# One query chunk of layer 0's second half is taken from the streamed place, and loads around it change their order and places

## The reference

```python
q = rmsnorm(qkv[..., :D]...); k = rmsnorm(qkv[..., D:2 * D]...); v = qkv[..., 2 * D:]
attn = p[:, :, 0] - lam * p[:, :, 1]            # two softmaxes a head
h = h + rmsnorm(attn @ v, sub_gain) * (1 - lam_init) @ w_o

q = (xt @ w_q).reshape(T, 8, 2, 128)            # PEER: 8 retrieval heads
s = einsum('thpd,hpkd->thpk', q, sub_keys)      # 128 keys in each half
s_top, i_top = top_k(s, 16); cand = all 256 sums of a head; best, pos = top_k(cand, 16)
gates = softmax(best); idx = i_top[half 0] * 128 + i_top[half 1]
act = gelu(u_tab[idx] . x) * gates; y = sum(act * v_tab[idx])
```

## Time and profile before

| | us |
|---|---|
| median of three runs | 1524.82 |
| profiled execution | 1526.51 |
| its span | 1524.5 |
| TensorE busy | 1347.4 |
| VectorE busy | 992.3 |
| ScalarE busy | 596.1 |
| GpSimd busy | 570.4 |

### The profile page before, as it was taken

The page is one execution under the profiler, slowest core; times in us unless marked ns, Lnnn a source line. Parts: engine busy times, 40 slices in busy tenths (PEclk is TensorE's granted clock), DMA queues, the critical chain, the costliest instruction groups (busy, mean ns, idle before and its releaser), DMA issues.

```text
span 1524.5 us, 12571 instructions
## 1 busy us (share of the span) xinstructions
PE 1347.4 (88%) x3294; PEld 573.2 (38%) x3294; DVE 992.3 (65%) x2411; ACT 596.1 (39%) x1805; POOL 570.4 (37%) x518
## 2 busy tenths in 40 slices
PE   9999899899878889889887899899979889877777
PEld 4444344344333334334332334343433333222222
DVE  4677877875656777456478546667567867764444
ACT  1334364643333434334334433343434344343333
POOL 0033334453323344344334434333434444343442
PEclk9999999999999999999999999999999999999999
DMA  9879999999999999999999999999999999999998
GB/s 390 342 290 421 359 424 419 421 415 420 423 422 424 416 415 395 422 420 414 422 411 408 420 420 420 420 406 422 409 421 419 414 416 421 413 408 422 421 420 334
DMA packets 85751, 621.82 MB, mean 408 GB/s; under 512 B 9520, under 2 KB 9648, under 8 KB 13104
## 3 DMA queue, kind: packets, MB, share of 16 engines
q0 software_dynamic: 74016, 536.90, 85.6%
q1 hardware_dynamic: 9936, 76.81, 12.2%
q10 hardware_dynamic: 1728, 7.31, 1.2%
HBM read 619.94 MB, written 1.05 MB: 407 GB/s over the span
## 4 chain that ended last, share of the span: by engine, by line
DMA 42%; PE 33%; DVE 13%; ACT 7%; issue 4%; POOL 1%; SPq 0%; DVEq 0%; POOLq 0%; ACTq 0%
DMA ring<-in_peer_uv_dram,idx 41%; PE acc L649 22%; PE pp L397 9%; DVE ring L1460 7%; ACT diag L993 2%; DMA ring<-in_w_qkv_dram 2%; ACT weight L989 1%; ACT L987 1%; ACT gelu L987 1%; ACT L850 1%; POOL ring L764 1%; PE tt L412 1%; ACT work L813 1%; DVE top_i L1177 1%; DVE pick L1219 0%
## 5 line engine op out<-in xcount | busy, mean ns | idle before, releaser
L649 PE MATMUL acc<-ring,diag 128*128 128x512 f32 x2048 | 995.2, 611 | 165.9 <-ACT diag L993 161.3
L1460 DVE CUSTOM_DVE_ANT_0 ring<-ring,xf 128x1024 f32<-128x1024 f32 x512 | 627.1, 1226 | 456.5 <-DMA ring<-in_peer_uv_dram,idx 447.2
L764 POOL DMA_INDIRECT ring<-in_peer_uv_dram,idx x510 | 566.2, 1110 | 937.4 <-PE acc L649 828.4
L649 PEld LDWEIGHTS acc<-ring,diag 128*128 128x128 f32 x2048 | 371.0, 191 | 726.0 <-ACT diag L993 383.6
L987 ACT ACTIVATE gelu<-dots 128x1 f32<-128x1 f32 x512 | 103.6, 202 | 803.4 <-DVE dots L1460 803.0
L993 ACT ACTIVATE diag<-const,weight 128x128 f32<-128x128 f32 x512 | 205.4, 401 | 16.8
L989 ACT ACTIVATE weight<-gelu,gates 128x1 f32<-128x1 f32 x512 | 150.8, 294 | 16.6
L397 PE MATMUL pp<-stream,xT 128*128 128x512 f32 x160 | 81.1, 596 | 0.0
L397 PE MATMUL pp<-stream,rows 128*128 128x512 f32 x96 | 49.0, 592 | 0.0
L397 PEld LDWEIGHTS pp<-stream,xT 128*128 128x128 f32 x160 | 30.4, 194 | 36.0 <-issue 36.0
L1460 DVE DVE_READ_ACCUMULATOR2_ANT dots<- 128x1 f32 x512 | 42.0, 82 | 0.0
(11 more groups left out here) (165 smaller groups left out, 763.8 us busy)
## 6 DMA issues: line engine op xcount, KB each, us to landing
stream<-in_peer_w_q_dram SPq DMA_DIRECT2D x18, 1024.0 KB, 9.4
stream<-in_conv_w_in_dram SPq DMA_DIRECT2D x12, 1024.0 KB, 9.4
ring<-in_peer_uv_dram,idx POOLq DMA_INDIRECT x510, 10.4
stream<-in_w_qkv_dram SPq DMA_DIRECT2D x4, 1024.0 KB, 11.9
ring<-in_w_qkv_dram SPq DMA_DIRECT2D x2, 2048.0 KB, 26.8
stream<-in_w_o_dram SPq DMA_DIRECT2D x4, 1024.0 KB, 18.5
kept<-in_peer_w_q_dram SPq DMA_DIRECT2D x2, 2048.0 KB, 11.5
ring<-in_w_qkv_dram SPq DMA_DIRECT2D x2, 1024.0 KB, 11.7
```

What stands on the lines that cost most here:

```text
L649: mm = nc.tensor.matmul(acc[half][:, :], diag[:, s % RING, :], row[:, D + half * 512:D + (half + 1) * 512], start=(k == 0), stop=(k == SLO ...
L764: nc.gpsimd.indirect_dma_start(dst, None, uv_dram, bass.IndirectOffsetOnAxis(idx[:, at:at + 1], 0)).then_inc(landed, 16)
L1460: nc.vector.tensor_tensor_reduce(row[:, 0:D], row[:, 0:D], xf[:, s // SLOTS % 2, :], 1.0, 0.0, ALU.mult, ALU.add, dots[:, s % RING:s % RIN ...
```

## The change

Query chunk 2 of layer 0 stays in the streamed place for both halves, as chunk 3 stays in `kept`. The second half ranks chunks 2 and 3 (heads 4 to 7) first and then 1 and 0 (`QUERY_ORDER`), and its gathers run over the heads in this order. For that, half 1's key chunk 1 is projected at slot 25 (was 41), query chunk 2 of half 0 at slot 33 (was 25), value chunk 1 at slot 41 (was 33) and query chunk 3 at slot 55 (was 50). The second output chunk of half 1 is loaded to place 6, where the V rows were, and its first four matmuls are due at slot 80 (was 72). Layer 1's first loads stand in another order and ahead of the second half's query chunks. The normalisation of key chunk 1 uses another scratch area and no longer waits for a transpose. The functions `chunk_of` and `reader_after` map a position to the chunk and to the reader.

```diff
--- before.py
+++ after.py
@@ -66,7 +66,7 @@
     dict(q0=12, k0=22, q1=30, k1=54,
          logits0=25, bias0=26, max0=30, exp0=31, diff0=35, turn0=38, values0=42,
          logits1=57, bias1=58, max1=62, exp1=63, diff1=68, turn1=71, values1=75,
-         norm0=45, norm1=77, gain=54, y0=49, y1=81, out00=68, out10=72, out01=84, out11=88, h0=88, f0=90, h1=92, f1=94, scale=93,
+         norm0=45, norm1=77, gain=54, y0=49, y1=81, out00=68, out10=80, out01=84, out11=88, h0=88, f0=90, h1=92, f1=94, scale=93,
          wq0=94, wq1=104, wq2=112, wq3=120),
     dict(x=2, in2=6, in4=14, in3=22, in5=30, in0=38, in1=46, z0=23, z1=39, turn_z0=25, turn_z1=41, turn_g0=49, turn_g1=57,
          conv0=28, conv1=44, gain=20, times0=52, times1=59, out00=60, out10=64, out01=68, out11=72, h0=72, f0=74, h1=76, f1=78,
@@ -77,17 +77,23 @@
 )
 SECOND_HEAD = 0
 FIRST_NORM = 8
-LATE_RANK_PROJECT = {1: 0, 2: 25, 3: 50}
+LATE_RANK_PROJECT = {1: 0, 2: 33, 3: 55}
+QUERY_ORDER = {1: (2, 3, 1, 0)}
 RANK_AT = {(1, 2): 133, (1, 3): 149}
 HALF = KT // 2
 RANK_PIECES = {(0, 1): 2, (0, 2): 2, (0, 3): 1, (1, 0): 2}
-LATE_IN_PROJECT = {2: 9, 1: 17, 5: 33, 3: 41}
-SHARED = {(1, "in", 0), (1, "in", 4), (1, "in", 5), (1, "out", 0), (1, "wq", 3),
+LATE_IN_PROJECT = {2: 9, 1: 17, 3: 25, 5: 41}
+SHARED = {(1, "in", 0), (1, "in", 4), (1, "in", 5), (1, "out", 0), (1, "wq", 0), (1, "wq", 1),
           (3, "in", 2), (3, "in", 3), (3, "in", 5), (3, "out", 0), (3, "out", 1), (3, "wq", 2), (3, "wq", 3)}
 PARTS = 2
 DEEP = KT // PARTS
 WARM = 3
 
+
+
+def chunk_of(n, what, c):
+
+    return QUERY_ORDER[n][c] if what == "wq" and n in QUERY_ORDER else c
 
 
 def pieces(n, c):
@@ -293,9 +299,9 @@
             places[2 + i] = ring[:, 2 * i:2 * i + 2, :].rearrange("p r d -> p (r d)")
         loads = [(0, "in", 0, 4), (0, "in", 2, 5), (0, "in", 1, STREAM), (0, "in", 3, 3), (0, "in", 4, 2), (0, "in", 5, 7),
                  (0, "out", 0, 8), (0, "out", 1, STREAM), (0, "wq", 0, 5), (1, "in", 2, HOLES), (1, "in", 1, 9), (0, "wq", 1, STREAM)]
-        loads += [(0, "wq", 2, STREAM), (1, "in", 3, STREAM), (0, "wq", 3, 7),
-                  (1, "out", 1, STREAM), (1, "wq", 0, STREAM), (1, "wq", 1, STREAM), (1, "wq", 2, STREAM)]
-        loads += [(2, "in", 2, 6), (2, "out", 0, 8), (2, "in", 4, STREAM), (2, "in", 3, 7), (2, "out", 1, 9), (2, "in", 5, 10), (2, "in", 0, STREAM),
+        loads += [(1, "in", 3, STREAM), (0, "wq", 2, STREAM), (0, "wq", 3, 7), (1, "out", 1, 6)]
+        loads += [(2, "out", 1, 9), (2, "out", 0, 8), (2, "in", 2, 6), (1, "wq", 2, STREAM), (2, "in", 3, 7), (1, "wq", 3, STREAM),
+                  (2, "in", 4, STREAM), (2, "in", 5, 10), (2, "in", 0, STREAM),
                   (2, "in", 1, STREAM), (2, "wq", 0, STREAM), (2, "wq", 1, STREAM)]
         loads += [(3, "in", 4, STREAM), (2, "wq", 2, 6), (2, "wq", 3, 7), (3, "in", 0, STREAM), (3, "in", 1, STREAM),
                   (3, "wq", 0, STREAM), (3, "wq", 1, STREAM)]
@@ -338,7 +344,13 @@
 
         def held(n, what, c):
 
-            return held_at[(n - 1 if (n, what, c) in SHARED else n, what, c)]
+            if (n, what, c) in SHARED:
+                return held_at[n - 1, what, chunk_of(n, what, c)]
+            return held_at[n, what, c]
+
+        def reader_after(n, what, c):
+
+            return next(((n + 1, what, later) for later in range(6) if (n + 1, what, later) in SHARED and chunk_of(n + 1, what, later) == c), None)
 
         def weights(n, what, c, k):
 
@@ -397,7 +409,7 @@
                     mm = nc.tensor.matmul(bank[:, 0:width], src[:, k, :], weights(n, what, c, k)[:, columns], start=(k == 0), stop=(k == KT - 1))
                     if k == KT - 1:
                         mm.then_inc(pool.written_sem(key), 1)
-                    elif k % DEEP == DEEP - 1 and held(n, what, c)[0] == STREAM:
+                    elif k % DEEP == DEEP - 1 and held(n, what, c)[0] == STREAM and reader_after(n, what, c) is None:
                         mm.then_inc(part_used, 1)
 
             def project(pool, n, what, c, src, at, ks=range(KT)):
@@ -469,7 +481,7 @@
                 key = (n, "score" + part, c)
                 bank = take(ss, key)
                 for j in range(2 * js[0], 2 * js[0] + 2 * len(js)):
-                    mm = nc.tensor.matmul(bank[:, j * P:(j + 1) * P], qT[:, j, :], keysT[:, 4 * c + j, :], start=True, stop=True)
+                    mm = nc.tensor.matmul(bank[:, j * P:(j + 1) * P], qT[:, j, :], keysT[:, 4 * chunk_of(n, "wq", c) + j, :], start=True, stop=True)
                 mm.then_inc(ss.written_sem(key), 1)
 
             def front():
@@ -653,8 +665,8 @@
                 mm.then_inc(v_used, 1)
 
             front()
-            sides = begun(late(1), late_input(2), turn_late("q", 0), late_input(1), turn_late("k", 0), attention(0), late(2),
-                          turn_late("q", 1), late_input(5), late_input(3), turn_late("k", 1), late(3), turn_mixed(0), attention(1), turn_mixed(1),
+            sides = begun(late(1), late_input(2), turn_late("q", 0), late_input(1), turn_late("k", 0), attention(0), late_input(3),
+                          turn_late("q", 1), late(2), late_input(5), turn_late("k", 1), late(3), turn_mixed(0), attention(1), turn_mixed(1),
                           output(1), turn_output(1), *(experts(1, c) for c in range(4)))
             for n in (2, 3):
                 sides += begun(gated_input(n), turn_gated(n), output(n), turn_output(n), *(experts(n, c) for c in range(4)))
@@ -669,12 +681,12 @@
         @block.sync
         def _(sp):
             def matrix_of(n, what, c):
-                return {"in": in_dram[n // 2], "out": out_w_dram[n // 2], "wq": peer_w_q[n // 2]}[what][c]
+                return {"in": in_dram[n // 2], "out": out_w_dram[n // 2], "wq": peer_w_q[n // 2]}[what][chunk_of(n, what, c)]
 
             def last_reader(n, what, c):
 
-                if (n + 1, what, c) in SHARED:
-                    n = n + 1
+                if reader_after(n, what, c):
+                    return reader_after(n, what, c)
                 return n, "wqb" if (n, what, c) == (0, "wq", 0) else what, c
 
             def load_first():
@@ -994,7 +1006,7 @@
 
             front()
             sides = begun(second_head(), late(1), late_input(2), turn_late("q", 0), late_input(1), turn_late("k", 0), attention(0),
-                          late(2), turn_late("q", 1), late_input(5), late_input(3), turn_late("k", 1), new_gain(1), late(3), turn_mixed(0),
+                          late_input(3), turn_late("q", 1), late(2), late_input(5), turn_late("k", 1), new_gain(1), late(3), turn_mixed(0),
                           attention(1), turn_mixed(1), output(1), *(experts(1, c) for c in range(4)), new_keys())
             for n in (2, 3):
                 sides += begun(gated_input(n), turn_gated(n), new_gain(n), output(n), *(experts(n, c) for c in range(4)))
@@ -1081,9 +1093,7 @@
 
                 copied(dve, pool, (n, "in", c))
                 src = mixed_rows(n, c).rearrange("p (c d) -> p c d", d=DH)
-                if (n, c) == (1, 3):
-                    written(dve, tt, (1, "attn", 1))
-                square_groups(src, 8, DH, rows[:, 0:CHUNK] if n == 1 and c < 3 else scratch[:, 0:CHUNK])
+                square_groups(src, 8, DH, rows[:, 0:CHUNK] if n == 1 else scratch[:, 0:CHUNK])
                 yield
                 rsqrt_of_mean(8, DH, root[:, 0:8])
                 yield
@@ -1462,7 +1472,7 @@
 
             front()
             sides = begun(*(finish(n) for n in range(WINDOWS - 1)))
-            sides += begun(second_head(), first_norm(), late_input(2), late(1), late_input(1), attention(0), late(2), late_input(3), late(3), attention(1),
+            sides += begun(second_head(), first_norm(), late_input(2), late(1), late_input(1), attention(0), late_input(3), late(2), late(3), attention(1),
                            output(1), *(experts(1, c) for c in range(4)))
             for n in (2, 3):
                 sides += begun(gated_input(n), convolve(n), output(n), *(experts(n, c) for c in range(4)))
```

## The result

The kernel after takes 1527.2 us (median of 20 runs) against 1524.97 us of the kernel before on the same chip: ratio 1.0015 [1.0009, 1.0021], 2.2 us slower. The forecast was 1522.2 us, 2.6 us faster. The profiled execution took 1530.85 us with a span of 1529.0, 3.6 us over the median of its own runs; places in the traces are read from single executions, times from the medians.

The account below looks back on a forecast made before the run. DMA bytes were taken as the first bound, with TensorE's pace almost equal in stretches without weight loads. The terms -5.0 + 2 + 0.4 = -2.6 us took the median from 1524.82 to 1522.2 us; range 1519.5 to 1527.5.

Parts of the forecast that it names:

- Part 1: Six weight chunks of 2.097 MB fetched instead of seven in this part of the list: 5.0 us gained at 421 GB/s.
- Part 2: Loads leave 200 to 245 us, so the DMA idles there: 2 us taken, between 0.9 and 3.6.
- Part 3: Heads 4 and 5 ranked at slots 46 to 53 instead of 38 to 45: cost 0.4 us, bounds 0 and 5.6.
- 1 to 2 of waits: Slots 55 to 68: TensorE's waits in us, added to 32.6 us of work, so slot 68 starts at 296 to 298.
- part 5: Loads moved to slots 79 to 92, DMA-bound still: 0, up to 1 us; key normalisation at slots 34 to 36: 0.
- Part 4: Short leads of query chunks and second output chunk before their use: 0 each, up to 1 us for some.
- The key normalisation, 0: 4 us of VectorE at slots 34 to 36, beside 4.48 us of waiting for ScalarE's exponentials: cost 0.
- Rival 3: VectorE becomes the bound in slots 46 to 76, slot 55 is 3.8 us late: 1528.6 us; chance 0.16.
- rival 2: Gain eaten: ranking and the exponentials after it keep slot 68 at 300 us, time 1524.8 us; chance 0.20.
- Rival 4: TensorE's clock falls in a wait for VectorE, 1.7 us per group of four add matmuls: 1523.9 us; chance 0.08.
- The two signs: Forecast wrong if slot 68 starts after 300 us, or more than 2.4 us of idling shows before slot 76.

Follow-up runs that it names:

- e3: Kernel after, but query chunk 2 is not shared and is fetched once more (2.097 MB, asked for at slot 75): 1532.88 us, 1.0052 of before.
- e2: Kernel after, with VectorE's normalisation of key chunk 1 begun at slot 37 instead of 34: 1525.39 us, 1.0001 of before.
- e8: Kernel after, with the second output chunk's first four matmuls due at slot 82 instead of 80: 1527.98 us, 1.0021 of before.
- e12: Kernel after, with value chunk 1 at slot 44, query chunk 3 at 57, heads 6 and 7 ranked from 72, normalisation in slot 34: 1525.7 us, 0.9997 of before.
- e10: e2 with value chunk 1 at slot 44, query chunk 3 at slot 57, heads 6 and 7 ranked from slot 72: 1523.15 us, 0.9986 of before.
- e6: Kernel after, with normalisation of key chunk 1 from slot 37 and ranking of heads 6 and 7 from slot 71: 1526.2 us, 1.0006 of before.
- e9: e2 with the projection of query chunk 3 at slot 53 instead of 55: 1525.5 us, 1.0002 of before.
- e11: e2 plus 2.1 MB of extra loads, asked for from slot 35 on and used by nothing: 1524.74 us, 0.9997 of before.

## Why the prediction was wrong, step by step

- **Part 1**, 5.0 us for a chunk: right as a size (5.7 in e3), wrong as to where it is earned. It was booked as a gain of the whole, to be reduced by idling; the balance of bytes on either side of slot 68 was not drawn.
- **Part 2**, 2 us of idling in 200 to 245: the mechanism was right, the size not. 200 to 243 moved 378 GB/s, an unused 4.4 us, more than the high end of 3.6. With the normalisation out of the way, e2, it is 2.4 in 220 to 250.
- **Part 3**, this step failed, in its term of "1 to 2 of waits". Slot 68 came at 303.56, predicted 296 to 298. From slot 55 to slot 68 TensorE took 40.66 us, where 32.6 of work and 1 to 2 of waits had been added up. It waited 5.6 us, each time for ScalarE's diagonals, 4.2 of it at the two blocks of exponentials, and was busy 35.0, 0.9 of it by a lower clock. The 5.5 us of idling in 243 to 300 us, which the prediction took for room, were mostly such waits: 4.9 us stood between slots 55 and 68 before, 3.8 of them at the same two blocks. They were not used up; TensorE's idling in 243 to 300 grew to 8.9 us. The cost was not 0.4 us; 4.3 went unused in 290 to 330. Slot 55 came at 262.90 where 262.7 was predicted, and that was luck: e2, without the wait in slot 34, has it at 261.11, so that a count 1.6 us too slow covered the 1.8 us of part 5.
- **Part 4**: the output chunk waited 3.25 us in slot 80 where 0 was said, and nothing is won without that wait (e8). It landed 12.3 us after it was asked for at 322.71, against a predicted 11.2; and without the wait slot 80 had come at 331.9, so that the lead was 9.2 us and not 12.5.
- **Part 5**: saturated from slot 76 on, near enough (422 GB/s in 330 to 505, all of it; 403 in 315 to 330). "The key normalisation, 0" was wrong, and is the largest single cause that the runs show: it was put beside VectorE's wait of 4.48 us, but it does not use that wait, it lengthens it to 7.78, since its input is a copy queued on ScalarE behind the same exponentials. e2 prices it at 1.8 us, e12 against e10 at 1.7. Each is no more than the uncertainty of such a difference, but they agree, and in both pairs the add ahead of slot 68 moves with it (1.8 and 1.85 us).
- **Rivals.** Rival 3 named the price and the point rightly, every us by which slot 68 starts after 300: 3.6 us late, 1528.4 by its rule, 1527.2 measured. Its mechanism was another one: slot 55 was 1.6 us late and not 3.8, and VectorE was not too busy (29.18 of 40 us in 290 to 330, down from 36.43). Nearer to the cause was what rival 2 had for it, TensorE idle in 290 to 295 beside the exponentials. Rival 4 came too, for 0.9 us in the profiled execution. The two signs that were named as refuting the forecast, slot 68 after 300 us and more than 2.4 us of idling, both came. That 1527.2 lies in the range is no merit of the sum: its slow end was there for rival 3.

e6 and e9, with slot 68 at 300.7, are not faster than e2 with 302.0, since the three do not differ ahead of the clock's fall: their adds start at 298.88, 298.84 and 299.05. What stays open is where the rest of the 2.7 us comes from by which the add ahead of slot 68 was late: the normalisation explains 1.8, and no run here separates the remaining 0.9.

## What to carry to other kernels

Where a stretch bound by the engines is followed by one bound by the DMA, draw the balance of bytes on either side of the border: here only bytes behind it, and the moment at which it is reached, counted. When a step moves, look for what makes its input and what is queued ahead of that on its engine; a wait is no free place for a step whose input stands in the same queue behind what is waited for. Idle time of an engine is room only if what it waits for moves too: look at the releaser. Before a wait is blamed, see whether the next engine ran dry by it; the longest one here, 7.01 us, did not reach TensorE. A stretch may need a gap in one engine's side work more than an earlier start (e10).

## What the runs showed of the hardware

The DMA's busy share did not tell of the loss, the GB/s did. Four windows of the kernel after:

```profile
225.00:230.00 5.00, 5.00 (x28) 3.33 (x27) 3.37 (x5) 0.60 (x1) 1.07 (x1) 1.00 1.01 362
230.00:235.00 5.00, 5.00 (x14) 2.26 (x13) 1.86 (x11) 2.17 (x7) 1.87 (x2) 1.00 0.86 297
240.00:245.00 5.00, 5.00 (x13) 2.17 (x12) 4.79 (x23) 1.43 (x6) 1.75 (x2) 1.00 1.01 329
305.00:310.00 5.00, 5.00 (x13) 2.17 (x12) 4.43 (x15) 0.90 (x3) 1.06 (x2) 0.99 0.82 247
```

At a share of 1.01 the core moved 362 and 329 GB/s, 14% and 22% less than the 421 that go with the same share elsewhere.

TensorE's clock can fall in the wait before slot 68, and need not. In 300 to 305 us TensorE was granted 0.69 in e2 and 1.00 in e11 (last but two of the columns), and slot 68 came at 302.00 and 300.54:

```profile
300.00:305.00 5.00, 5.00 (x9) 2.11 (x8) 4.49 (x20) 1.83 (x7) 0.99 (x1) 0.69 0.70 251
```

```profile
300.00:305.00 5.00, 5.00 (x13) 2.26 (x12) 4.83 (x20) 1.62 (x7) 2.26 (x2) 1.00 1.00 403
```

The group of four add matmul records before slot 68, in e2 and then in e11, after the same wait:

```profile
299.05 3.15 PE L661 MATMUL acc<-ring,diag 128*128 128x512 f32 x4 [2.41 <-ACT diag L1005]
```

```profile
298.72 1.98 PE L662 MATMUL acc<-ring,diag 128*128 128x512 f32 x4 [2.41 <-ACT diag L1012]
```

A granted 0.69 is partly at 1.2 GHz. The group took 1.17 us longer, of the 1.46 us by which slot 68 differs: rival 4's fall (1.7 us for a group), at the place where TensorE is the bound. These are single executions. From the start of that group to slot 68 it takes 1.82 us in six of the fourteen traces and 2.3 to 3.6 in the other eight (columns "add" and "slot 68" of the table), so a slot 68 that moves by less than 1.8 us tells nothing by itself. The Trainium skill, "TensorE: Matmul & The Clock Gate", section "HAM oscillation", puts the fall down to waits between bursts; the wait of 2.41 us went with it in e2 and without it in e11.
